# Decoder step on one core: the output projection turned round, and one gating step moved ahead of the pooling unit

## What is computed

```python
rq, rk, rv, rg, nq, ck, cv, sk, sv, wk, wv, gl = _project(x, w_in)      # 2048 -> 6680
ret_out = silu(rg) * group_norm(chunk_retention(rope(rq), rope(rk), rv))
o = sigmoid(gl)[0] * o_cmp + sigmoid(gl)[1] * o_sel + sigmoid(gl)[2] * o_win
feats = concatenate([ret_out, o], -1)
h = _layer_norm(DEEPNORM_ALPHA * x + feats @ w_o, ln1_g, ln1_b)
g_logit = h @ w_group + b_group          # 4 groups
e_logit = h @ w_expert + b_expert        # 8 experts in each group, top 2 of the chosen group
# y: sum over the two experts of gate * (silu(h @ w_gate[e]) * (h @ w_up[e])) @ w_down[e]
return _layer_norm(DEEPNORM_ALPHA * h + y, ln2_g, ln2_b)
```

## Time and profile before

| | us |
|---|---|
| median of 3 runs | 1953.94 |
| lowest, highest | 1948.2, 1954.58 |
| the profiled execution, its own time | 1955.87 |
| its span in the trace | 1954.0 |
| phase_f, from the start | 0 to 538 |
| phase_s | 538 to 677 |
| phase_m, projection to routing | 677 to 907 |
| phase_m, experts and last norm | 907 to 1954 |

### The profile page before, as it was taken

One profiled execution on the slowest core, in us unless ns is written; L12 is line 12 of the kernel. 1 busy time (PEld: TensorE's weight loads), 2 busy tenths in 40 slices (PEclk: granted clock), 3 DMA queues, 4 the chain that ended last, 5 costly groups with the idle time before them and its releaser, 6 DMA issues.

```text
span 1954.0 us, 17953 instructions
## 1 busy us (share of the span) xinstructions
PE 1545.7 (79%) x7566; PEld 845.4 (43%) x7566; DVE 489.3 (25%) x896; ACT 208.2 (11%) x449; POOL 140.1 (7%) x152
## 2 busy tenths in 40 slices
PE   4999998898588789855987777887878787877770
PEld 3787777677466433343332323232323232323220
DVE  0724566476444111234000000000000000000007
ACT  0013210110153100010000000000000000000010
POOL 2100010110110000000000000000000000000000
PEclk9999999999898889956999998989999999999995
DMA  9975486785789696313999999999999999999963
GB/s 277 313 235 184 159 266 195 214 254 155 292 309 377 241 384 255 129 45 132 405 406 407 407 407 409 414 407 412 414 407 412 398 407 390 403 405 407 405 268 136
DMA packets 218818, 612.67 MB, mean 314 GB/s; under 512 B 19217, under 2 KB 145713, under 8 KB 160529
## 3 DMA queue, kind: packets, MB, share of 16 engines
q1 hardware_dynamic: 192352, 503.55, 68.7%
q0 software_dynamic: 16960, 84.76, 11.5%
q10 hardware_dynamic: 9416, 23.08, 3.2%
HBM read 607.70 MB, written 36.42 MB: 330 GB/s over the span
## 4 chain that ended last, share of the span: by engine, by line
DMA 44%; PE 16%; DVE 4%; SPq 1%; issue 0%; ACT 0%; POOLq 0%; DVEq 0%; ACTq 0%
DMA arena<-in_w_up 42%; PE ps L1666 6%; PE ps L1723 6%; PE ps L1740 1%; PE ps L1669 1%; PE ps L1683 1%; DVE arena L1644 1%; SPq L1365 1%; PE ps L1678 1%; DMA arena<-in_w_o 1%; DMA arena<-y_rows 0%; DVE arena L1646 0%; DVE arena L1503 0%; DVE arena L1652 0%; DVE arena L1504 0%
## 5 line engine op out<-in xcount | busy, mean ns | idle before, releaser
L1723 PE MATMUL ps<-arena 128*64 128x512 f32 x2048 | 504.0, 642 | 184.7 <-DMA arena<-in_w_up 183.4
L642 PE MATMUL ps<-arena 128*128 128x264 f32 x1664 | 389.4, 393 | 29.1 <-DMA arena<-in_w_in 29.1
L1723 PEld LDWEIGHTS ps<-arena 128*64 128x64 f32 x2048 | 171.5, 147 | 516.0 <-issue 514.0
L642 PEld LDWEIGHTS ps<-arena 128*128 128x128 f32 x1664 | 318.1, 194 | 84.9 <-issue 28.0
L1624 DVE TENSOR_TENSOR arena<-arena,ps 64x512 f32<-64x512 f32 x32 | 22.1, 692 | 903.7 <-ACT arena L1453 903.7
L1740 PE MATMUL ps<-arena 128*64 128x512 f32 x1024 | 228.5, 599 | 16.5 <-ACT arena L1455 16.5
L1740 PEld LDWEIGHTS ps<-arena 128*64 128x64 f32 x1024 | 71.1, 137 | 150.2 <-issue 129.2
L1666 PE MATMUL ps<-arena 128*128 128x512 f32 x256 | 117.1, 611 | 13.8 <-DMA arena<-in_w_o 13.8
L1405 POOL DMA_INDIRECT y_rows<-arena,keep x32 | 32.1, 1002 | 927.8 <-ACT arena L1460 927.8
L1453 ACT ACTIVATE arena<-ps 64x512 f32<-64x512 f32 x32 | 18.9, 589 | 636.6 <-PE ps L1723 636.6
L1666 PEld LDWEIGHTS ps<-arena 128*128 128x128 f32 x256 | 48.4, 194 | 81.9 <-issue 81.9
(11 more groups left out here) (380 smaller groups left out, 894.8 us busy)
## 6 DMA issues: line engine op xcount, KB each, us to landing
arena<-in_w_gate SPq DMA_DIRECT2D x128, 1024.0 KB, 28.5
arena<-in_w_up SPq DMA_DIRECT2D x128, 1024.0 KB, 29.2
arena<-in_w_down SPq DMA_DIRECT2D x128, 1024.0 KB, 29.4
arena<-in_w_in SPq DMA_DIRECT2D x52, 1024.0 KB, 6.9
arena<-in_w_o SPq DMA_DIRECT2D x16, 1024.0 KB, 14.5
arena<-in_w_cmp_k POOLq DMA_DIRECT2D x8, 512.0 KB, 7.0
arena<-in_w_cmp_v POOLq DMA_DIRECT2D x8, 512.0 KB, 7.0
arena<-in_win_k SPq DMA_DIRECT2D x8, 512.0 KB, 6.0
```

The costliest lines, as they stand in the source:

```text
L642: last = pe.matmul(ps[:, n % 2, 0:T], ring[:, n % FRONT_SLOTS, k, :], x[:, k, :], start=(k == 0), stop=(k == KT - 1))
L1723: last = [pe.matmul(ps[BS * u:BS * u + BS, 0, :], xs[:, k, :], ring[:, slots[u], kk * CHUNK:(kk + 1) * CHUNK], start=(k == 0), stop=(k == ...
```

## The change

1. **phase_f.** `gated(2r)` moves from the next round's j = 0, where it stood behind the pooling unit of j = 7, to j = 7 ahead of that unit. The 32 units are spread otherwise: one more before tile 11, one at each of j = 7, 0, 1, 2, 3, 4, none at 5 and 6 (before: two at j = 4 and none at j = 0).
2. **Projection.** Chunk c of w_o is now 128 output columns with all 16 k tiles, in pieces of 512 bytes. PE keeps the weights stationary and moves all 264 tokens, so the sum comes out transposed; DVE adds ALPHA x to it in that form (x_t is loaded in place of x).
3. **Early logits.** One chunk behind, `from_tile` turns the columns back into rows (three transposes, two copies on ACT, three statistics on DVE) and adds the chunk's part of the router's logits, from the sum before the norm with weights that are multiplied by the gain. The gain and shift vectors make two correction columns, in four steps on PE set between products of chunk 1: `affine_turned`, `bias_column`, `scale_column`, `spread_columns`. When mean and variance are known the logits are corrected by small operations.
4. **The norm.** h gets only mean and variance, on ACT (three operations on 128x2048), beside the routing. Gain and shift are applied to the gathered rows in their transposed form, two operations in `turned` in place of one copy, and to the residual in two halves (`residual`, ahead of experts 2 and 4), for which ACT loads ln1_g and ln1_b in four transfers of 0.5 MB ahead of experts 1 and 3. Before, they were two transfers of 1 MB at the start of phase_m.

```diff
-                if late and j == 0:
-                    gated(2 * r - 2)
                 if n < N_TILES and v_reads[n]:
                     rope_full(n)
...
                 if late and j == 7:
                     normed(2 * r + 1)
+                    gated(2 * r)
                 if late and j == 0:
                     gated(2 * r - 1)
...
-                units = 1 if 2 <= n < 10 else (0, 1, 1, 1, 2, 0, 0, 1)[j] if R_TILE < n < N_TILES else 0
+                units = 1 if 2 <= n < 11 or R_TILE < n < N_TILES and j not in (5, 6) else 0
...
             for c in range(n_wo):
-                n4, q = c // 4, c % 4
-                sp.dma_start(ring[:, c].rearrange("p (k n) -> p k n", k=4),
-                             w_o[:, 4 * q:4 * q + 4, n4 * CHUNK:(n4 + 1) * CHUNK]).then_inc(full[c], 16)
+                sp.dma_start(ring[:, c].rearrange("p (k n) -> p k n", k=KT), w_o[:, :, c * P:(c + 1) * P]).then_inc(full[c], 16)
...
+            for n in range(KT):
+                act.wait_ge(S["c_tr"], n + 1)
+                cols_n = slice(n * P, (n + 1) * P)
+                A.copy(h[:, 0:2, cols_n], ps[:, 2 + n % 2, 0:2 * P].rearrange("p (t c) -> p t c", t=2))
+                A.copy(h[0:NS_TOK, 2, cols_n], ps[0:NS_TOK, 2 + n % 2, 2 * P:3 * P]).then_inc(S["c_rows_in"], 1)
...
+            for t, (t0, n) in enumerate(TOK):
+                A.activation(h[0:n, t], h[0:n, t], ACT.Identity, bias=shift[0:n, t:t + 1], scale=rstd[0:n, t:t + 1]).then_inc(S["c_h"], 1)
...
             for e in range(NE):
+                if e in (1, 3):
+                    act.wait_ge(S["d_ln_free"], e // 2 + 1)
+                    for j, name in enumerate(("ln1_g", "ln1_b")):
+                        act.dma_start(ln1[:, j, :], a[name][:, e // 2 * D // 2:(e // 2 + 1) * D // 2].broadcast_to([P, D // 2])).then_inc(S["d_ln"], 16)
                 expert(e)
...
+            for n in range(KT):
+                if n % 4 == 0:
+                    v.wait_ge(S[f"c_x{n // 4}"], 16)
+                v.wait_ge(S["used"], n + 1)
+                v.scalar_tensor_tensor(ht[:, n, :], ht[:, n, :], ALPHA, ps[:, n % 2, 0:T], ALU.mult, ALU.add).then_inc(S["c_hp"], 1)
+                if n >= 2:
+                    row_stats(n - 2)
...
             def turned(e):
                 v.wait_ge(S["d_xt"], e + 1)
-                v.tensor_copy(xs.rearrange("p (a k) s -> p a (k s)", a=2), ps[:, 2:4, :]).then_inc(S["d_xs"], 1)
...
+                v.tensor_tensor(xs, turned_rows, per_row(0), ALU.mult).then_inc(S["d_xm"], 1)
+                v.wait_ge(S["d_xm"], e + 1)
+                v.tensor_tensor(xs, xs, per_row(1), ALU.add).then_inc(S["d_xs"], 1)
...
+            def from_tile(n):
+                pe.wait_ge(S["c_hp"], n + 1)
+                if n >= 2:
+                    pe.wait_ge(S["c_rows_in"], n - 1)
+                for t, (t0, rows) in enumerate(TOK):
+                    last = pe.transpose(ps[0:rows, 2 + n % 2, t * P:(t + 1) * P], ht[:, n, t0:t0 + rows], ident)
+                last.then_inc(S["c_tr"], 1)
+                last = pe.matmul(ps[0:n_lg, 4, 0:T], w_r[:, n, :], ht[:, n, :], start=(n == 0), stop=(n == KT - 1))
...
+            for n in range(KT):
+                pe.wait_ge(full[n], 16)
...
+                for k in range(KT):
+                    last = pe.matmul(ps[:, n % 2, 0:T], ring[:, n, k * P:(k + 1) * P], xt[:, k, :], start=(k == 0), stop=(k == KT - 1))
...
+                    if n >= 1 and k == (13 if n == 1 else 7):
+                        from_tile(n - 1)
+                last.then_inc(S["used"], 1)
```

More of the change, by code:

```diff
@@ L1434, in _ @@
[L1434 to L1441, removed]
@@ L1479, in _ @@
             done = m.dve
[L1480 to L1495, removed]
@@ L1496, in _ @@
[L1496 to L1504 removed]
+            done.link(v.memset(agg, 1.0))
@@ new lines, in _, with row_stats @@
+            last.then_inc(S["c_diag"], 1)
+            v.wait_ge(S["c_spread"], 1)
+            v.tensor_copy(spread[:, 0], ps[:, 5, 128:128 + n_lg])
+            v.tensor_tensor(spread[:, 1], ps[:, 5, 128 + n_lg:128 + 2 * n_lg], bias, ALU.add)
+            def row_stats(n):
+                v.wait_ge(S["c_rows_in"], n + 1)
+                for t, (_, rows) in enumerate(TOK):
+                    last = v.bn_stats(stats[0:rows, t, n, :], h[0:rows, t, n * P:(n + 1) * P])
+                return last
@@ L1510, in _ @@
+            done.link(last)
+            v.tensor_tensor(shift, shift, rstd, ALU.mult).then_inc(S["c_h"], 1)
+            for t, (_, n) in enumerate(TOK):
+                last = v.scalar_tensor_tensor(lg[0:n, t], lg[0:n, t], rstd[0:n, t:t + 1], spread[0:n, 1], ALU.mult, ALU.add)
             done.link(last)
@@ L1624, in expert, with residual @@
                 v.tensor_tensor(hb[BS:P, :], hb[BS:P, :], ps[BS:P, 0, :], ALU.mult).then_inc(S["d_hb"], 1)
+            def residual(part):
+                half = slice(part * D // 2, (part + 1) * D // 2)
+                v.wait_ge(S["d_ln"], 32 * (part + 1))
+                v.wait_ge(S["c_hst"], 48)
+                for t, (_, n) in enumerate(TOK):
+                    done.link(v.scalar_tensor_tensor(h[0:n, t, half], h[0:n, t, half], ALPHA, ln1[0:n, 0], ALU.mult, ALU.mult))
+                    last = v.scalar_tensor_tensor(h[0:n, t, half], ln1[0:n, 1], ALPHA, h[0:n, t, half], ALU.mult, ALU.add)
+                last.then_inc(S["d_ln_free"], 1)
             turned(0)
-            v.wait_ge(S["c_hst"], 48)
-            for t, (_, n) in enumerate(TOK):
-                v.tensor_scalar(h[0:n, t], h[0:n, t], ALPHA, None, ALU.mult)
+            v.sem_inc(S["d_ln_free"], 1)
             for e in range(NE):
+                if e in (2, 4):
+                    residual(e // 2 - 1)
                 expert(e)
@@ new lines, in bias_column, with scale_column @@
+            def bias_column():
+                pe.wait_ge(S["c_gb"], 1)
+                for k in range(KT):
+                    last = pe.matmul(ps[0:n_lg, 5, 65:66], w_r[:, k, :], gb_r[:, 1, k:k + 1], start=(k == 0), stop=(k == KT - 1))
+                last.then_inc(S["c_bcol"], 1)
+            def scale_column():
+                pe.wait_ge(S["c_gw"], 1)
+                for k in range(KT):
+                    last = pe.matmul(ps[0:n_lg, 5, 64:65], w_r[:, k, :], r_("ones")[:, 0:1], start=(k == 0), stop=(k == KT - 1))
+                last.then_inc(S["c_cols"], 1)
@@ new lines, in spread_columns @@
+            def spread_columns():
+                pe.wait_ge(S["c_diag"], 1)
+                for j in (0, 1):
+                    last = pe.matmul(ps[:, 5, 128 + j * n_lg:128 + (j + 1) * n_lg], r_("ones", n_lg), diag[0:n_lg, j], start=True, stop=True)
+                last.then_inc(S["c_spread"], 1)
+            def from_tile(n):
[6 more added lines that the diff above has]
+                last = pe.matmul(ps[0:n_lg, 4, 0:T], w_r[:, n, :], ht[:, n, :], start=(n == 0), stop=(n == KT - 1))
+                if n == KT - 1:
+                    last.then_inc(S["c_lt"], 1)
@@ L1681, in _ @@
+            from_tile(KT - 1)
+            pe.wait_ge(S["c_lt_in"], 1)
             for t, (t0, n) in enumerate(TOK):
-                for k in range(KT):
-                    last = pe.matmul(ps[0:n, 2 + t, 0:NG + NE], ht[:, k, t0:t0 + n], w_r[:, k, :], start=(k == 0), stop=(k == KT - 1))
+                last = pe.matmul(ps[0:n, 5, t * n_lg:(t + 1) * n_lg], lg_t[0:n_lg, t0:t0 + n], ident[0:n_lg, 0:n_lg], start=True, stop=True)
             last.then_inc(S["c_lg"], 1)
```

120 lines of the change are left out of this document (69 added, 51 removed).

## The result

The changed kernel took **1868.03 us** (median of four runs, 1864.98 to 1869.72), the kernel before 1954.26 (1948.2 to 1961.99): ratio 0.954, 95% interval 0.9507 to 0.9572. The prediction was 1877, in a range of 1863 to 1897. The profiled execution has a span of 1863.1 us where the one of before had 1954.0, 90.9 less.

The account below looks back on a forecast made before the run. The full-DMA expert stage starts with the first expert, behind phase_m's one chain; phase_f was bound by PE's waits for DVE. Phase_f 44 and phase_m 34 less make 78 off 1955.9, predicted median 1877 us, range 1863 to 1897.

Parts of the forecast that it names:

- the forecast 78: Whole kernel: 44 us less in phase_f and 34 less in phase_m, taken off the profiled execution's 1955.9 us.
- -44 forecast: Phase_f: PE's waits for gated and states go, 34.8 us over three rounds and 8.9 in the tail.
- The bound of 50: Phase_f: largest gain allowed, 50 us, with no wait at all and a little more from the rounds' start.
- (a): Phase_m, first chunk of w_o: 512-byte pieces move slower, 292 against 391 GB/s; +3 us, between 0 more and 16.6 in all.
- (b): Phase_m, projection loop: 135 us after 132, +3, with from_tile at 0.8 us each and correction steps at 6 us.
- (c): Phase_m, last chunk to routing: some 20 small steps, 5 us, replace 51.6 us; 46.6 less, bounds 42 and 48.
- (d): Phase_m, routing: stays 33.6 us; ACT's norm of h, 6.7 us, hides beside it with 11 us of cover.
- (e): Phase_m, first expert: the second operation in turned costs +1.3 us; later ones lie behind the DMA.
- the price of +5.2: Full stage: four half transfers of ln1_g and ln1_b, 2.1 MB at 407 GB/s, cost 5.2 us while DMA is full.
- Rival 4: Expert stage: residual waits for its rows, making the kernel slower if each lands over 92 us after issue; chance 0.02.
- Rival 2: Projection: w_o slices come slower than PE needs; at 100 GB/s the loop takes 168 us, +33, 1910; chance 0.05.
- Rival 3: End of phase_f: stores and page loads end last at the barrier and take back 20 us, 1897; chance 0.05.

Follow-up runs that it names:

- gated_only: Kernel before with only the gating step moved ahead of the pooling unit, the table of units as before: 1927.98 us, ratio 0.9858.
- units_only: Kernel before with only the new places of the pooling units, the gating step still behind the unit of j = 7: 1935.82 us, ratio 0.99.
- before_x_late: Kernel before with all of ACT's phase_m loads issued only once the first chunk of w_o has landed: 1945.39 us, single time.
- logits_late: Changed kernel with all sixteen from_tile and all row statistics after the projection's last product: 1867.36 us, ratio to before 0.9542.
- more_rows: Changed kernel with 512 KB more of broadcast rows loaded for each expert but the first, into a tile nothing reads: 1909.53 us, once.
- one_step: Changed kernel with the four steps of the correction vectors in one block after the second chunk's second product, not spread over that chunk: 1874.02 us, once.

## Why the prediction was right, and where a step was off

The median came 9 us below the forecast of 1877 and 5 above the lower end of the range. The errors did not cancel: of the 12.8 us by which the traces gained more than the forecast 78, 5.6 lie in phase_f, 5.4 at the first chunk, 2.1 in phase_s and 1.6 in the full stage, and only 1.9 lie the other way.

**Phase_f, -44 forecast, -49.6 in the trace.** The mechanism was right: both waits gone, rounds of 61.57 us against 61.5 worked out, last round to L751 25.7 against 25.9, clock near 1.00. Two terms were too small. I took 1 us of waits for each round, and there were none (the bound of 50 said so); and the first round's start is the same, so 3 x 12.5 = 37.5 against 34.8. The other lies past the last L751. I left the way to the barrier as it was; it went from 12.95 to 9.65 us. The landing times of the last store of ACT, before and after:

```profile
L450 ACTq DMA_DIRECT2D out_p_ret<-arena x1: 437/437/437, 529.5 to 529.5; - x1
...
DMA to landing us min/median/max: 7.5/7.5/7.5
```

```profile
L450 ACTq DMA_DIRECT2D out_p_ret<-arena x1: 437/437/437, 483.1 to 483.1; - x1
...
DMA to landing us min/median/max: 3.6/3.6/3.6
```

Before, DVE's last unit ended ahead of L753, and with it SP's six loads of win_k went out at 524.7, 3 us ahead of the stores that the barrier waits for. With `gated` first the unit ends later, and the loads go out at 484.3, 1.2 us behind the last store. gated_only has the short way too (5.6 us from the last store's issue to phase_s) and units_only the long one (9.0), so it comes with `gated`'s place. That the loads ahead are the cause is read from the order and was not tried.

**Phase_s, 0 forecast, -2.1.** Not an effect that can be told: in the fourteen traces of this study, all with the same phase_s, it lasted 132.4 to 139.5 us. The prediction should have carried some 3 us of such scatter.

**Phase_m.** (a) The failed step is "In 512-byte pieces DMA moved 292 GB/s ... I take +3": it was -2.4. Piece size was made the price, and the loads issued beside the chunk were named only for the lower bound ("less is loaded beside it"); before_x_late shows them to be 7.2 of 12.3 us. (b) The loop, +3.9 for +3: from_tile cost 1.07 us against 0.8, 4 us more in fifteen. The correction steps' products are two blocks of 1.28 us where I had 5.3 for both, and with no waits, which gave most of that back. (c) 5.93 us for the forecast 5, as worked out. The early place of the logits was not what mattered, see logits_late: one block behind the projection, with PE busy and at full clock ahead of it, does as well. (d) ACT's norm (2.1 us for each of three, 6.3 against 6.7) hid as forecast. (e) +1.3 as forecast.

**In the full stage** the price of +5.2 was right by more_rows (5.5), the trace has +3.6. Rival 4 was far off: the halves of ln1_g, on ACT's queue, landed after 8.1 and 8.3 us and those of ln1_b, behind them, after 13.1 and 13.4, not after 28.5 as SP's. Rival 2 fell with PE's one wait for w_o, for the first chunk; the later ones streamed at 290 GB/s against the 131 needed. Rival 3 was opposite to what the barrier did, which took 3.3 us less.

## What to carry to other kernels

When a stretch gets shorter by moving work, run the new work at the old place: here the rewriting of norm and logits gave 42 us from the first product to the routing (183.6 to 141.9), and the early place of the logits nothing. Price a wait of TensorE with what follows it: the products behind it can go at the lower clock (2.9 us behind 2.0 us of waits in one_step). And at the start of a phase look at what is issued in the same microsecond as the transfer that PE waits for; in the kernel before it cost 7.2 of the 12.3 us.

## What I had not expected of the hardware

- Three waits of 0.4 to 0.9 us within 5 us were followed by 3.2 us at a granted clock of 0.50 (one_step).
- Loads issued 3 us or more behind a transfer left its landing alone (12.4 us with them and 12.3 without, 10.05 and 9.8); 2.1 MB issued with it, and 0.6 MB close behind, made the first product 7.2 us later.
- Products with one moving column took 0.038 us per instruction (two blocks of 32 in 1.21 us each up to the next), under half of the 0.083 that I scaled from the logits of before.
- A stage without any edit (phase_s) scattered by 7 us over fourteen traces, with PE's granted clock between 0.86 and 0.90 and DMA's share between 0.85 and 0.92.
